# Turning all four merged column blocks on VectorE

## What is computed

```python
for layer in range(2):
    h = rms_norm(x, pre_g)
    proj = h @ w_in                       # 2048 -> 12 x 1536 + 3 x 2048 columns
    o_a, o_c, o_r = attention(..), conv(..), retention(..)     # each 256 x 1536, gated
    merged = (sigmoid(g_a) * (o_a @ w_branch_a)
              + sigmoid(g_c) * (o_c @ w_branch_c)
              + sigmoid(g_r) * (o_r @ w_branch_r))             # 256 x 2048
    y = merged @ w_out
    x = x + rms_norm(y, post_g)
```

## Time and profile before

| | |
|---|---|
| three runs | 2750.38, 2750.63, 2750.84 us; median 2750.63 |
| the profiled execution | 2750.84 us; its span, first to last instruction, 2749.0 us |
| TensorE busy | 2734.5 us, 99% of the span, 12264 matmuls and transposes |
| VectorE busy | 1924.1 us, 70% |
| ScalarE busy | 1221.9 us, 44% |
| mean granted TensorE clock | 0.999 of full speed |

### The profile page before, as it was taken

The page is one execution under the profiler, slowest core; times in us unless marked ns, Lnnn a source line. Parts: engine busy times, 40 slices in busy tenths (PEclk is TensorE's granted clock), DMA queues, the critical chain, the costliest instruction groups (busy, mean ns, idle before and its releaser), DMA issues.

```text
span 2749.0 us, 30429 instructions
## 1 busy us (share of the span) xinstructions
PE 2734.5 (99%) x12264; PEld 2269.6 (83%) x12264; DVE 1924.1 (70%) x2556; ACT 1221.9 (44%) x1402; POOL 25.9 (1%) x35
## 2 busy tenths in 40 slices
PE   9999999999999999999999999999999999999998
PEld 7888888888888888888878888888888888888887
DVE  5778754767645898848567887447776558977584
ACT  5454544444443333444454545444444433434443
POOL 0000000000000000000000000000000000000000
PEclk9999999999999999999999999999999999999999
DMA  8555556556556555556565555565665565555663
GB/s 317 183 184 185 178 190 199 190 193 198 189 195 195 187 174 179 184 197 216 184 230 184 178 190 174 196 196 184 200 198 190 192 198 173 192 173 183 199 215 138
DMA packets 264732, 529.10 MB, mean 192 GB/s; under 512 B 8464, under 2 KB 8848, under 8 KB 264336
## 3 DMA queue, kind: packets, MB, share of 16 engines
q1 hardware_dynamic: 260976, 517.50, 57.1%
q10 hardware_dynamic: 2608, 4.78, 0.5%
q0 software_dynamic: 1008, 4.87, 0.5%
HBM read 522.94 MB, written 4.19 MB: 192 GB/s over the span
## 4 chain that ended last, share of the span: by engine, by line
PE 99%; DVE 0%; DMA 0%; ACT 0%; issue 0%; DVEq 0%; POOL 0%; SPq 0%; POOLq 0%
PE ps L633 32%; PE ps L635 32%; PE ps L634 32%; PE ps L569 0%; PE ps L589 0%; PE ps L587 0%; PE ps L586 0%; PE ps L565 0%; DMA raw<-w_in 0%; PE ps L550 0%; PE ps L570 0%; PE ps L564 0%; DVE w_trail L877 0%; DVE gates L1147 0%; DVE hT_trail L1118 0%
## 5 line engine op out<-in xcount | busy, mean ns | idle before, releaser
L877 DVE TENSOR_TENSOR w_trail<-raw,w_lead 128x1024 fp32r<-128x1024 f32 x975 | 1190.9, 1224 | 771.0 <-ACT w_lead L698 761.5
L698 ACT ACTIVATE w_lead<-raw 128x1024 fp32r<-128x1024 f32 x975 | 1030.7, 1060 | 1404.3 <-PE ps L635 1400.8
L633 PE MATMUL ps<-w_lead,hT_lead 128*128 128x512 f32 x3328 | 1299.8, 391 | 4.9 <-DVE w_trail L877 3.9
L635 PE MATMUL ps<-w_lead,hT_trail 128*128 128x512 f32 x3328 | 1296.1, 389 | 0.0
L634 PE MATMUL ps<-w_trail,hT_lead 128*128 128x512 f32 x3328 | 1295.8, 389 | 0.0
L633 PEld LDWEIGHTS ps<-w_lead,hT_lead 128*128 128x128 f32 x3328 | 625.5, 188 | 135.3 <-issue 5.8
L635 PEld LDWEIGHTS ps<-w_lead,hT_trail 128*128 128x128 f32 x3328 | 625.2, 188 | 129.9
L634 PEld LDWEIGHTS ps<-w_trail,hT_lead 128*128 128x128 f32 x3328 | 625.5, 188 | 129.0
L633 PE MATMUL ps<-w_lead,oT_lead 128*128 128x512 f32 x576 | 224.3, 389 | 0.0
L635 PE MATMUL ps<-w_lead,oT_trail 128*128 128x512 f32 x576 | 224.1, 389 | 0.0
L634 PE MATMUL ps<-w_trail,oT_lead 128*128 128x512 f32 x576 | 224.1, 389 | 0.0
(11 more groups left out here) (100 smaller groups left out, 774.8 us busy)
## 6 DMA issues: line engine op xcount, KB each, us to landing
raw<-w_in SPq DMA_DIRECT2D x381, 1024.0 KB, 5.1
raw<-w_out SPq DMA_DIRECT2D x32, 1024.0 KB, 5.1
raw<-w_branch_a SPq DMA_DIRECT2D x24, 1024.0 KB, 5.0
raw<-w_branch_c SPq DMA_DIRECT2D x24, 1024.0 KB, 5.1
raw<-w_branch_r SPq DMA_DIRECT2D x24, 1024.0 KB, 5.0
raw<-w_in SPq DMA_DIRECT2D x5, 512.0 KB, 7.8
gates<-x SPq DMA_DIRECT2D x4, 512.0 KB, 12.6
post_gain<-post_norm_g POOLq DMA_DIRECT2D x2, 1024.0 KB, 7.4
```

The costliest lines, as they stand in the source:

```text
L633: pe.matmul(acc, lead[:, k, tok(t)], wl, start=(k == 0), stop=False)
L635: last = pe.matmul(acc, trail[:, k, tok(t)], wl, start=False, stop=(k == BLOCKS[n][2] - 1))
L698: act.activation(w_lead[:, h % SPLIT_SLOTS, :], raw[:, i % RAW_SLOTS, part:part + HALF * COLS], ACT.Copy).then_inc(lead_ready, 1)
L877: dve.tensor_tensor(w_trail[:, s, :], raw[:, i % RAW_SLOTS, part:part + HALF * COLS], w_lead[:, s, :].bitcast(F32), ALU.subtract).then_inc ...
```

## The change

`MERGE_TURNED` becomes 4: TensorE transposes nothing of `merged` any more, and the two PSUM splits behind its transposes are gone. VectorE turns all four blocks. Blocks 2 and 3 use `kT` and `qT` again, behind a wait for the trails of blocks 0 and 1. Block 2 is cut into six pieces as blocks 0 and 1 are; the last block has three pieces of 6, 5 and 5 instructions in the slots h0+4, h0+5 and h0+6; its lead stands in slot h0+6 and its trail in slot h0+7. Block 2's lead stands in slot h0+4 and its trail in slot h0+5.

```diff
-MERGE_TURNED = 2
+MERGE_TURNED = OUT_BLOCKS
...
-MERGE_TURN_DUE = {MERGE_AT[j] + i + AHEAD: (j, i) for j in range(MERGE_TURNED) for i in range(len(TURNS))}
-MERGE_LEAD_DUE = {MERGE_AT[j] + len(TURNS) + AHEAD: j for j in range(MERGE_TURNED)}
+MERGE_TURNS = [TURNS] * (OUT_BLOCKS - 1) + [((0, 6), (6, 11), (11, 16))]
+MERGE_TURNED_BY = [sum(map(len, MERGE_TURNS[:j + 1])) for j in range(OUT_BLOCKS)]
+MERGE_TURN_DUE = {MERGE_AT[j] + i + AHEAD: (j, i) for j in range(OUT_BLOCKS) for i in range(len(MERGE_TURNS[j]))}
+MERGE_LEAD_DUE = {MERGE_AT[j] + len(MERGE_TURNS[j]) - (j == OUT_BLOCKS - 1) + AHEAD: j for j in range(OUT_BLOCKS)}
...
-                        act.wait_ge(merged_turned, len(TURNS) * (MERGE_TURNED * l + j + 1))
+                        act.wait_ge(merged_turned, MERGE_TURNED_BY[-1] * l + MERGE_TURNED_BY[j])
...
+                        if piece == 0 and j > 1:
+                            dve.wait_ge(merged_trail, TILES * (MERGE_TURNED * l + j - 1))
-                        a, b = TURNS[piece]
+                        a, b = MERGE_TURNS[j][piece]
                         for n in range(a, b):
                             last = dve.transpose(
-                                square_of((kT, qT)[j], n % QUADS, n // QUADS, TILES),
+                                square_of((kT, qT)[j % 2], n % QUADS, n // QUADS, TILES),
```

## The result

The changed kernel takes 2768.61 us (median of four runs, 2767.91 to 2768.93), the kernel before 2750.51 us beside it: a ratio of 1.0065, 95% interval 1.0052 to 1.0078, or 18.1 us more. The forecast was 2768.8.

What follows compares the result with a forecast made beforehand. TensorE, busy 99% of the span, was taken to bound the kernel. Per layer, waits of 8.4 and 2.5 us less 1.8 us of transposes give +9.1, twice +18.2 on 2750.63: 2768.8 us, range 2765 to 2774.6.

Steps and rivals of the forecast that it cites:

- What bounds the kernel, and what leaves TensorE's list: TensorE, busy 99%, bounds the kernel; removing two groups of eight transposes a layer saves 0.90 us each, 3.6 in all.
- VectorE's list, replayed: From the split of h0-2, VectorE runs without pause; block 2's trail ends at 1303.49, block 3's at 1311.46 us.
- The first wait: At h0+4 TensorE waits 8.4 us a layer for block 2's trail.
- The second wait and the clock: At h0+6 TensorE waits 2.5 us for block 3's trail; this covers the low clock's 1.6 us, counted as 0.
- the last rival: Block 2's trail comes earlier, first wait 2.1 us; the sum still follows block 3's trail date alone; chance 0.07.
- The sum: Per layer +8.4 + 2.5 - 1.8 = +9.1 us, paid in two layers: +18.2 us.
- The clock's rival: Low clock outlasts the second wait's cover or falls again behind it: 1.6 to 2.9 us more a layer; chance 0.13.
- Not slower: VectorE's trails come in time, only the removed transposes count: 2747.0 us, within 0.2%; chance 0.05.
- one wait: Block 2's trail is earlier, first wait 2.1 us; only a shorter VectorE list, 1.2 us a layer, gives 2766.4; chance 0.07.

Runs made afterwards that it cites:

- e6: Kernel before the change, with TensorE's 16 transposes of merged per layer issued twice; median 2.0 us more, ratio 1.0010.
- e1: Changed kernel with block 2's trail written right behind the split of half h0+4, ahead of block 3's turning pieces; 2772.22 us, ratio 1.0079 to the kernel before.
- e7: e1 with nine unread constant products filling TensorE's wait ahead of half h0+6; 2767.61 us, ratio 1.0062 to the kernel before.
- e4: Changed kernel with halves of the first two output column blocks taken in turn, and blocks 2 and 3 turned in eight and four pieces; 2747.92 us.
- e8: e4 with block 3 turned in six pieces of 3, 3, 3, 3, 2 and 2 instead of four of 4; 2748.94 us.
- e5: Kernel before the change with only e4's order of halves, blocks 2 and 3 still transposed by TensorE; 2749.93 us, ratio 0.9999.

## Why the prediction was right, step by step

- *What bounds the kernel, and what leaves TensorE's list.* Right: h0 starts at 16.32 and not 17.22 us, 0.90 a group, and e6 measures 0.88 for the same eight instructions.
- *VectorE's list, replayed.* From the split of h0-2 to the end of block 2's trail I had 1303.49 - 1276.19 = 27.3 us; the trace has 1302.17 - 1275.07 = 27.1. To the end of block 3's trail 35.27 predicted, 35.11 in the trace. The small rest has a source: I took 1.26 us from a split to the turning behind it each time, but for a block's first piece it is 1.15 (1293.52 to 1294.67). The 1.06 us of one split by ScalarE is not in the earlier trace rows, which show 1.99 for two; the trace after has lead and split together at the predicted 2.13 (1305.62 to 1307.75).
- *The first wait.* 8.4 us predicted. From h0+4's own date, 1275.07 + 19.07 = 1294.14, to its start at 1302.23 are 8.1; besides the 0.2 above, the matmul follows the trail by 0.06 us and not by 0.15.
- *The second wait and the clock.* I expected the low clock to cost 1.6 us and the second wait to take in up to 2.5 of it. It cost 2.9 us in layer 0, which used the second wait up (no wait is left, and h0+6 starts at 43.68 us for 43.55 predicted), and 2.0 in layer 1, where 0.42 us of wait remain (43.30). So the size of this term was 0.4 to 1.3 us too low, and the date of block 3's trail hid nearly all of the error. That this date alone makes the sum stood in the last rival as an argument; e1 has shown it.
- *The sum.* h0+6 starts 9.2 and 8.8 us later than before, 9.1 predicted. That the median came within 0.2 us of the forecast is luck beyond this: its interval is 14.3 to 21.5 us more, and small errors of opposite sign met (the replay was 0.2 us a layer too long, and in layer 0 the low clock lasted longer than the second wait could take in).
- *The rivals.* The clock's rival (the low clock outlasts the second wait) is true in part: in layer 0 h0+6 starts 0.4 us later than in layer 1, and 0.2 us of it are left at h0+8 (49.12 against 48.89). "Not slower" is out. So is "one wait": the first wait is 7.93 us and VectorE's list 0.2 us shorter than predicted, not 1.2; and where block 2's trail is written early there is still the whole loss (e1).
- *The rules of the Trainium skill.* That an idle gap brings the clock down (TensorE: Matmul & The Clock Gate, "Why this matters for your kernels") agrees with all four long waits of e1 and of the changed kernel: granted 0.50 in the slow stretches of the changed kernel, and 0.60 and 0.66 in the longer stretches read behind e1's, which take in some time at full speed. e7 is the same wait without the idleness, at 1.00. Not every gap did it: behind 3.19 us at the start of the changed kernel's program the clock stayed up (below). The advice of the Trainium skill to transpose 128x128 on TensorE (VectorE: DVE Perf Modes, "Rules for kernel authors") is right at these dates, but e4 shows that it is the date that decides: with room ahead of it, VectorE's 7.0 us a block replace TensorE's 0.9 at a gain.

What stays open: whether e4 can be brought to the full 3.6 us. This would need a split or a piece placed better between h0+6 and h0+12; e8 is the one attempt at it.

## What to carry to other kernels

Before work is moved to an engine with idle time, write down the date at which its result is needed and replay that engine's list up to it, from start to start, with everything that stands ahead in its order; the average idle share (30% here, with no pause for 30 us at the place in question) says nothing about it, and neither does an engine's share of the chain. Where two waits of one engine follow each other and the later date does not move, removing the earlier wait gains nothing; in e1 it even cost 4 us, because the low clock was then no longer covered. To use an idle engine, move the date first, as e4 does, and check by a kernel with the new order alone (e5) that the room costs nothing.

## What the runs showed of the hardware that I had not expected

- How long the clock stays down behind a wait is not the same from one wait to the next. Behind two waits of 7.93 us in one execution TensorE was slow from 1302.23 to 1307.9 and from 2679.93 to 2683.5, which cost 2.9 and 2.0 us.
- The start of the program varies nearly as much as the change could have gained: in the ten profiled executions half h0-6 of layer 0 starts between 1265.60 and 1268.32 us. Before the second half of the weights TensorE waited 3.39 us in the profiled execution of the kernel before, with a slow stretch behind it, and 3.19 us in the one after, with none, so that half h0-6 started at 1268.06 and 1266.93 us. This part is the same in both kernels; 1.1 us of the difference between two profiled spans comes from there (the spans differ by 17.1 us, the stages by 18.2). The length of the wait alone does not tell which it will be: in e5's execution it is 2.88 us, with a slow stretch behind it (granted 0.55 from 13.40 to 16.90 us). The wait of the changed kernel:

```profile
13.09 0.47 PE L635 MATMUL ps<-w_lead,hT_lead 128*128 128x512 f32 x1 [3.19 <-DVE w_trail L879]
13.40 0.40 PE L636 MATMUL ps<-w_trail,hT_lead 128*128 128x512 f32 x1
```

- A VectorE transpose whose input or output starts in another quadrant of partitions (a group of 32) than that of the instruction ahead starts later: 1.26 us behind a split, and 1.15 where both start in the first quadrant (each block's first piece). In e4 a piece whose output starts in the first quadrant and only its input does not is at 1.25 (1300.12 to 1301.37). That the quadrant is the cause is read from the timelines only, and was not tested.
